# Gelu by its tanh form, four fetches at a time, on VectorE and ScalarE

## The reference, cut to what matters

```python
g = jax.nn.softmax(top_s, axis=-1).astype(hb.dtype)
u = jnp.take(expert_u, idx, axis=0)
act = jax.nn.gelu(jnp.einsum("thkd,td->thk", u, hb))
vv = jnp.take(expert_v, idx, axis=0)
return jnp.einsum("thk,thkd->td", g * act, vv)
```

## Time and profile before

| | |
|---|---|
| median of 3 runs | 2028.38 us (2023.79 to 2033.21) |
| profiled execution | 2043.05 us, its span 2041.0 us |
| PE busy | 1634.1 us (80%) |
| VectorE busy | 1205.5 us (59%) |
| ScalarE busy | 721.4 us (35%) |
| DMA moved | 718.22 MB, mean 352 GB/s |
| of it the indirect fetches | 604.02 MB, 72.2% of 16 engines' span |
| chain that ended last | DMA 42%, PE 29%, VectorE 14%, issue 8%, ScalarE 4% |

### The profile page before, as it was taken

One profiled execution on the slowest core, in us unless ns is written; L12 is line 12 of the kernel. 1 busy time (PEld: TensorE's weight loads), 2 busy tenths in 40 slices (PEclk: granted clock), 3 DMA queues, 4 the chain that ended last, 5 costly groups with the idle time before them and its releaser, 6 DMA issues.

```text
span 2041.0 us, 22251 instructions
## 1 busy us (share of the span) xinstructions
PE 1634.1 (80%) x7437; PEld 784.4 (38%) x7437; DVE 1205.5 (59%) x3104; ACT 721.4 (35%) x2231; POOL 628.5 (31%) x584
## 2 busy tenths in 40 slices
PE   6999998977887789889889677676676776767776
PEld 4775786844443345445355321121121121211221
DVE  2425112787787675544677667777766666665554
ACT  2215201353266543322423243333333333333332
POOL 0000000143331343333333254444343444343431
PEclk8999999998977799999999999998998999999989
DMA  9557520699995799999998699999999999999996
GB/s 399 205 189 269 194 91 21 247 375 362 395 366 220 291 411 421 421 421 411 414 389 322 253 423 421 421 422 421 422 421 421 421 422 421 422 420 422 422 420 249
DMA packets 100386, 718.22 MB, mean 352 GB/s; under 512 B 11488, under 2 KB 11504, under 8 KB 13488
## 3 DMA queue, kind: packets, MB, share of 16 engines
q0 software_dynamic: 82944, 604.02, 72.2%
q1 hardware_dynamic: 16464, 110.43, 13.9%
q10 hardware_dynamic: 864, 2.36, 0.3%
HBM read 712.04 MB, written 4.73 MB: 351 GB/s over the span
## 4 chain that ended last, share of the span: by engine, by line
DMA 42%; PE 29%; DVE 14%; issue 8%; ACT 4%; POOL 3%; SPq 0%; another core or an unknown queue 0%; DVEq 0%; POOLq 0%; ACTq 0%
DMA ring<-in_expert_uv_dram,uidx 41%; PE ps L877 7%; PE ps L612 6%; DVE ring L1544 6%; PE ps L736 4%; POOL ring L480 3%; PE ps L757 3%; PE ps L742 2%; DMA ring<-in_wpack_dram 1%; PE ps L608 1%; ACT wsel L1134 1%; PE ps L642 1%; PE ps L857 1%; ACT wdiag L1139 1%; DVE left L1447 1%
## 5 line engine op out<-in xcount | busy, mean ns | idle before, releaser
L877 PE MATMUL ps<-ring,wdiag 128*32 128x512 f32 x2304 | 814.1, 673 | 282.4 <-ACT wdiag L1139 206.6
L480 POOL DMA_INDIRECT ring<-in_expert_uv_dram,uidx x576 | 627.2, 1089 | 1328.8 <-PE ps L877 853.3
L1544 DVE CUSTOM_DVE_ANT_0 ring<-ring,mA 128x1024 f32<-128x1024 f32 x576 | 699.4, 1223 | 472.7 <-DMA ring<-in_expert_uv_dram,uidx 456.6
L877 PEld LDWEIGHTS ps<-ring,wdiag 128*32 128x32 f32 x2304 | 170.6, 118 | 846.1 <-ACT wdiag L1139 455.2
L1132 ACT ACTIVATE gel<-act_in 128x1 f32<-128x1 f32 x576 | 116.6, 202 | 854.7 <-DVE act_in L1544 839.8
L1139 ACT ACTIVATE wdiag<-repeat,wsel 128x32 f32<-128x32 f32 x576 | 185.1, 321 | 18.8
L1134 ACT ACTIVATE wsel<-gel,gsel 128x1 f32<-128x1 f32 x576 | 169.7, 295 | 18.7
L612 PE MATMUL ps<-hB,ring 128*128 128x320 f32 x320 | 93.1, 440 | 0.7 <-ACT convB L991 0.7
L612 PE MATMUL ps<-hA,ring 128*128 128x256 f32 x320 | 73.5, 391 | 6.8 <-DVE qB L1264 3.7
L795 PE MATMUL ps<-hB,ring 128*128 128x320 f32 x256 | 77.2, 455 | 0.0
L736 PE MATMUL ps<-hB,ring 128*128 128x320 f32 x256 | 73.2, 439 | 0.0
(11 more groups left out here) (241 smaller groups left out, 1593.7 us busy)
## 6 DMA issues: line engine op xcount, KB each, us to landing
ring<-in_wpack_dram SPq DMA_DIRECT2D x96, 1024.0 KB, 5.8
ring<-in_expert_uv_dram,uidx POOLq DMA_INDIRECT x576
xB<-in_x_b_dram SPq DMA_DIRECT2D x2, 1280.0 KB, 19.3
o_y_p<-mA ACTq DMA_DIRECT2D x16, 128.0 KB
xA<-in_x_a_dram SPq DMA_DIRECT2D x1, 1024.0 KB, 5.2
bias<-in_bias_dram SPq DMA_DIRECT2D x1, 1024.0 KB, 32.0
o_v_p<-kv SPq DMA_DIRECT2D x4, 256.0 KB, 13.4
o_k_p<-xB SPq DMA_DIRECT2D x4, 256.0 KB, 7.5
```

Source lines behind the costliest of these rows:

```text
L480: nc.gpsimd.indirect_dma_start(out=ring[:, slot, :], out_offset=None, in_=ins["expert_uv"], in_offset=bass.IndirectOffsetOnAxis(ap=uidx[:, ...
L877: mm = nc.tensor.matmul(pY[c * GT:(c + 1) * GT, half, :], wdiag[:, n % NDIAG, :], ring[:, ROW[n][0], D + half * 512:D + (half + 1) * 512], ...
L1544: nc.vector.tensor_tensor_reduce(r, r, h2n[:, g % 2, :], 1.0, 0.0, ALU.mult, ALU.add, act_in[:, g % 2, j:j + 1]).then_inc(s["dot"], 1)
```

## The change

The three ScalarE instructions of each fetch become work on a row of four fetches r (fetches 4r to 4r+3).

- VectorE, in entry 4r+3 behind the dot (`inner_row`): square, half of x times gate, factor, argument; four instructions on 128x4, two of them behind a wait for the one before.
- ScalarE, in entry 4r+4 (`tanh_row`): one Tanh on 128x4.
- VectorE, in entry 4r+4 behind the dot of fetch 4r+4 (`weight_row`): (tanh + 1) times half x times gate, one instruction on 128x4. It waits for the tanh.
- ScalarE, in entry 4r+5 (`spread_row`): the four diagonals, each as before.

TensorE, GpSimd, SyncE and the order are not touched. The folds of the row stay in TensorE's entry 4r+5. At the last row entry 576 has no dot. The buffers `gel` and `wsel` become two rows deep. ScalarE's waits for `placed_kept` go, since the dot of a row comes behind them anyway.

```diff
--- before.py
+++ after.py
@@ -20,6 +20,7 @@
 NKEY = 128
 TOPK = 16
 EPS = 1e-6
+GELU_A, GELU_C = 0.044715, 0.7978845608028654
 
 
 C_BADA, C_G1, C_G2, C_CW, C_CC, C_QG, C_KG, C_C = 0, 48, 56, 64, 76, 84, 85, 86
@@ -319,7 +320,7 @@
          "ada_ps", "ada_row", "ada_col", "mod", "x_loaded0", "x_loaded1", "x_again", "k_cache", "v_cache", "bias",
          "keys0", "keys1", "used",
          "shifted", "exp", "picked", "placed", "placed_kept",
-         "h2", "h2_kept", "dot", "gelu", "weight", "diag", "fold", "sum_kept", "joined", "scaled", "natural", "added", "stored",
+         "h2", "h2_kept", "dot", "inner", "tanh", "weight", "diag", "fold", "sum_kept", "joined", "scaled", "natural", "added", "stored",
          "gate_ps", "gate_sb", "v_out", "k_out", "state_ps", "state_row", "conv_out", "chain"]
 GROUP = ["sq", "sq_used", "mean", "inv", "root", "xn", "h_act", "h_dve", "z", "zsq", "zraw", "zsum", "zmean", "zinv", "zroot", "zqk", "za", "zd",
          "s_ps", "s_dve", "mx", "ex", "tp", "pt", "val", "on", "ot", "at", "kn_ps", "kn",
@@ -416,8 +417,8 @@
         uidx = sb("uidx", [P, 2, REP, GT], U32)
         gsel = sb("gsel", [P, 2, REP, GT])
         act_in = sb("act_in", [P, 2, GT])
-        gel = sb("gel", [P, GT])
-        wsel = sb("wsel", [P, GT])
+        gel = sb("gel", [P, 2, 4, REP])
+        wsel = sb("wsel", [P, 2, REP])
         wdiag = sb("wdiag", [P, NDIAG, GT])
         repeat = sb("repeat", [P, GT])
         stat = sb("stat", [P, 3, 2])
@@ -1121,23 +1122,18 @@
                         act.wait_ge(s["scaled"], GATED[n])
                     nc.scalar.copy(gate2, pG).then_inc(s["gate_sb"], 1)
 
-                def spread(n):
-                    g, j = n // GT, n % GT
-                    act.wait_ge(s["dot"], n + 1)
-                    p, a = TILES[g]
-                    if g == 0 and j % REP == 0:
-                        act.wait_ge(s["placed_kept"], nth(0, j // REP))
-                    if p and j == 0:
-                        act.wait_ge(s["placed_kept"], nth(p))
-                    nc.scalar.activation(gel[:, j:j + 1], act_in[:, g % 2, j:j + 1], ACT.Gelu_apprx_tanh).then_inc(s["gelu"], 1)
-                    act.wait_ge(s["gelu"], n + 1)
-                    nc.scalar.activation(wsel[:, j:j + 1], gel[:, j:j + 1], ACT.Identity,
-                                         scale=gsel[:, p % 2, a, j:j + 1]).then_inc(s["weight"], 1)
-                    act.wait_ge(s["weight"], n + 1)
-                    if n >= NDIAG:
-                        act.wait_ge(s["fold"], n - NDIAG + 1)
-                    nc.scalar.activation(wdiag[:, n % NDIAG, :], repeat[:, :], ACT.Identity,
-                                         scale=wsel[:, j:j + 1]).then_inc(s["diag"], 1)
+                def tanh_row(r):
+                    act.wait_ge(s["inner"], r + 1)
+                    nc.scalar.activation(gel[:, r % 2, 3, :], gel[:, r % 2, 2, :], ACT.Tanh).then_inc(s["tanh"], 1)
+
+                def spread_row(r):
+                    act.wait_ge(s["weight"], r + 1)
+                    for k in range(REP):
+                        n = REP * r + k
+                        if n >= NDIAG:
+                            act.wait_ge(s["fold"], n - NDIAG + 1)
+                        nc.scalar.activation(wdiag[:, n % NDIAG, :], repeat[:, :], ACT.Identity,
+                                             scale=wsel[:, r % 2, k:k + 1]).then_inc(s["diag"], 1)
 
                 def keep_sum(g):
                     act.wait_ge(s["fold"], GT * (g + 1))
@@ -1156,8 +1152,10 @@
                     act.dma_start(dst, prod[a * GT:(a + 1) * GT, :]).then_inc(s["stored"], 16)
 
                 def gather(n):
-                    if 1 <= n <= NG * GT:
-                        spread(n - 1)
+                    if n and n % REP == 0:
+                        tanh_row(n // REP - 1)
+                    if n > REP and n % REP == 1:
+                        spread_row(n // REP - 1)
                     m = n - 2
                     g, j = m // GT, m % GT
                     if j == 1 and g >= 1:
@@ -1544,6 +1542,26 @@
                     nc.vector.tensor_tensor_reduce(r, r, h2n[:, g % 2, :], 1.0, 0.0,
                                                    ALU.mult, ALU.add, act_in[:, g % 2, j:j + 1]).then_inc(s["dot"], 1)
 
+                def inner_row(r):
+                    g, j = r * REP // GT, r * REP % GT
+                    p, a = TILES[g]
+                    x, b = act_in[:, g % 2, j:j + REP], gel[:, r % 2]
+                    dve.wait_ge(s["dot"], REP * (r + 1))
+                    cd.did(nc.vector.tensor_tensor(b[:, 0, :], x, x, ALU.mult))
+                    cd.did(nc.vector.scalar_tensor_tensor(b[:, 1, :], x, 0.5, gsel[:, p % 2, a, j:j + REP], ALU.mult, ALU.mult))
+                    settle()
+                    cd.did(nc.vector.tensor_scalar(b[:, 0, :], b[:, 0, :], GELU_C * GELU_A, GELU_C, ALU.mult, ALU.add))
+                    settle()
+                    nc.vector.tensor_tensor(b[:, 2, :], b[:, 0, :], x, ALU.mult).then_inc(s["inner"], 1)
+
+                def weight_row(r):
+                    b = gel[:, r % 2]
+                    dve.wait_ge(s["tanh"], r + 1)
+                    if r >= 2:
+                        dve.wait_ge(s["diag"], REP * (r - 1))
+                    nc.vector.scalar_tensor_tensor(wsel[:, r % 2, :], b[:, 3, :], 1.0, b[:, 1, :],
+                                                   ALU.add, ALU.mult).then_inc(s["weight"], 1)
+
                 def scale(g):
                     p, a = TILES[g]
                     part = slice(a * GT, (a + 1) * GT)
@@ -1562,6 +1580,10 @@
                 def gather(n):
                     if n < NG * GT:
                         dot(n)
+                    if n < NG * GT and n % REP == REP - 1:
+                        inner_row(n // REP)
+                    if n and n % REP == 0:
+                        weight_row(n // REP - 1)
                     m = n - 2
                     g, j = m // GT, m % GT
                     if j == 7 and g >= 1:
```

## The result

The changed kernel takes 2152.90 us (median of 4 runs, 2146.05 to 2156.36) against 2030.80 us for the kernel before (median of 4, 2023.79 to 2045.03): a ratio of 1.0588, interval 1.0524 to 1.0652. It is slower by 122 us. The forecast was +45 and the range ended at 2105, so the direction held and the size did not.

What follows compares the result with a forecast made beforehand. Transfers bound the kernel from 1170 us, transfers and TensorE two earlier stretches, rounds of waits the other 395 us. Terms 8 + 5 - 5 + 10 + 25 + 2 = +45 on 2028.4 gave 2073 us; range 2020 to 2105.

Steps and rivals of the forecast that it cites:

- the refill: From 1170 us on, behind the last head: eleven slots with 6 us spare per row, so 0 us there.
- The time of a release: Every row: first fold 2.1 us behind the next row's dot, four folds over at 5.0, first slot free at 4.0.
- the bound of 16 us: Upper bound for 380 to 480 us: folds at the lower clock, taking twice as long.
- The cover of eight slots: 480 to 580 and 705 to 1000 us: transfers' cover falls to nothing, +5 (0 to 11) and +10 (0 to 24).
- rival C: The ring of slots runs dry, 24 and 11 us in the full stretches: +70, 2098 us; chance 0.12.
- The retrieval of group 1: 1000 to 1170 us: folds wait for dots behind a head's choice, delaying projections and `key_scores`: +25, bounds +8 and +33.
- the stand ahead of MAX8 in the fifth head: Retrieval of group 1: VectorE's wait ahead of the next choice would be longer than the 5.09 us before.
- The first heads: 380 to 480 us: folds behind the next dot delay `key_scores` 2.1 us a head for four heads: +8, bounds 0 and 16.
- Attention: 580 to 705 us: -10 table loads, -8 folds side by side, +10 later diagonals, +3 VectorE: -5, bounds -24 and above +10.
- rival D: Tanh needs its own table load after Exp, so 580 to 705 us stands at +5: 2083 us; chance 0.05.
- VectorE: Five small added instructions, about 0.9 us per four fetches, hidden behind 1170: +3 in attention, 2 in the retrieval.
- From 248 on: Fetches alone, paced by transfers: 0 us, plus 2 us behind the last dot for the last row.

Runs made afterwards that it cites:

- e11: The changed kernel with seven slots in turn for fetches instead of eight: 2263.73 us, ratio 1.1168 to the kernel before.
- e12: The changed kernel with nine slots for fetches instead of eight and two instead of three for weight blocks: 2109.40 us, ratio 1.0396 to the kernel before.
- e10: The changed kernel with TensorE's folds for fetches 188 to 227 moved from entry 4r+5 to 4r+7: 2119.39 us, ratio 1.0445 to the kernel before.
- e2: The kernel before with Tanh in place of Gelu, one fetch at a time, the rest of Gelu left out: 2034.21 us, ratio 0.9981.
- e5: The kernel before with five VectorE instructions added per row, writing a buffer that nobody reads: 2051.32 us, ratio 1.0070.

## Why the prediction was wrong in size

The mechanism and its place in the order were read rightly: no fold of a row ahead of the next dot, ring and `key_scores` behind it. No ACT_TABLE_LOAD is left in the attention stretch, as forecast. What failed is the sizes: the loss was put at 45 us and is 122, two of its terms came out above their upper bounds, and the refill, put at 0, at 14.

- **The time of a release.** The prediction had the first fold 2.1 us behind the dot, 2.9 us for four, the first slot free at 4.0 and the next issue at 4.3. Measured: 1.7 us to the first fold in most rows, a little better. Then there are two kinds of row. In the one the four folds take 1.9 to 2.5 us, and where the first starts at 1.7 the issue comes 3.9 us behind the dot, earlier than forecast. In the other, nearly always behind a stand of TensorE, they take 3.5 to 4.3 us, and the issue mostly comes at 5.2 to 6.1. From 88 to 184 eleven of 24 rows took over 3 us, from 184 to 232 ten of twelve; the mean from dot to issue is 4.9 and 6.1 us. So the step that failed is the price of a row of folds: the 1.94 us of the earlier trace rows is that of folds between projections, and it was used for rows that the change itself puts behind a stand. Only the bound of 16 us named the slower case, for the first stretch and no other. One row of each kind:

```profile
1021.61 2.54 PE L878 MATMUL ps<-ring,wdiag 128*32 128x512 f32 x16 [2.06 <-ACT wdiag L1135]
...
1023.78 1.56 POOL L481 DMA_INDIRECT ring<-in_expert_uv_dram,uidx  x1 [6.83 <-PE ps L878]
```

```profile
1714.07 3.89 PE L878 MATMUL ps<-ring,wdiag 128*32 128x512 f32 x16 [4.40 <-ACT wdiag L1135]
...
1717.92 1.45 POOL L481 DMA_INDIRECT ring<-in_expert_uv_dram,uidx  x1 [4.77 <-PE ps L878]
```

  In the first the issue comes 2.17 us behind the start of the folds, as forecast (1.9 + 0.3), in the second 3.85.
- **The cover of eight slots**, +10 for 88 to 184 and +5 for 24 to 56. Measured +19.0 and +11.5, rival C's mechanism (24 and 11). The 0.4 us a row was a choice, with the round of 11.7 us against 11.8 available. In the refill that round is 1275.50 - 1263.94 = 11.6 us, so it was right as a sum: a later release (5.6) met a shorter flight (6.0 instead of 7.4). The 7.4 was one reading and no floor; the trace of before has 6.2 us between fetches 100 and 183. But a round that equals what is available leaves nothing for rows that come late, and a mean over rows that vary lies above it. e11 and e12 show how steep it is here: +111 and -43 us for a slot.
- **The retrieval of group 1**, +25, measured +39.2. The effect was seen, but counted in full (8.1 us) for two heads and at 0.3 to 2 us for the others, whose rows "end in the dots anyway". In the trace of before nine of the twelve rows had begun to fold ahead of the next dot; two were read, and the rest was guessed. From one choice to the next (the first MAX8 of each head) the round of the second head takes 24.7 us instead of 16.0 and that of the fifth 25.1 instead of 19.4: +8.7 and +5.7 where 8.1 each was forecast. The other five rounds make +15.1, and the rows ahead of the first choice +9.8 (41.8 us from the dot of 184 instead of 32.0): 24.9 together, where 7 for the folds and 2 for VectorE were forecast. So it is less the two rows read than the rest. In the changed kernel TensorE stands 4.6 us or more in ten of twelve. One sign failed with it: the stand ahead of MAX8 in the fifth head is not longer than 5.09 us but 2.61, since VectorE now stands 6.05 us for fetch 216 first. e10 moves ten rows out of the way and gets 34.7 us of the stretch back.
- **The refill**, taken as 0 "from 1170", measured +14.0. This step was simply wrong: eleven slots are in turn only from fetch 237, and the first row there starts with an empty ring. The head of the stretch was read by its mean.
- **The first heads**, +8, measured +12.7. The four rounds that were priced, from the dot of 4 to that of 20, take 69.0 us instead of 60.1: +8.9, right as a size, though with folds of 4.1 us that begin 0.4 earlier. The rest is behind them, from the dot of 20 to that of 24 (11.7 us instead of 7.8): fetch 24 is issued at 483.73, and VectorE stands 4.79 us for its landing, where it stood none before. That is a slot that comes late, and the sum had no term for it.
- **Attention**, -5, measured +6.7. The loads were to give 10 us; the 45 that e2 removes in the whole kernel (68 were there, 23 are left), 58 us of ScalarE's time, give 2.3 us. So the chain's 8.2% was no saving; that the same engines waited for something else behind a load is the likely reason, and not shown. This also disposes of rival D, since Tanh needs no load of its own. The page "ScalarE: Activation LUTs" of the Trainium skill has the sharing of the table right ("Table sets: the hidden batching unit"), as e2's rows show. Its 2.66 us for a switch ("What ACT_TABLE_LOAD costs") is made of a load of about 1283 ns, which the rows show, and a drain, which they don't: there is 0.1 us of idle time ahead of eight loads. How attention's +6.7 is made up stays open: the parts here are as large as the difference between two executions.
- **VectorE**, +5 in all (3 in attention, 2 in the retrieval), measured +15 (e5). Its instructions cost 0.16 us each as forecast. e5's stretches differ from those of before by +3.7 in the first, +6.4 in attention and +2.8 in the last, the others by less or below nothing; with 5 us between executions, where the 15 lie isn't settled.
- **From 248 on**, 0, and 2 for the last row: measured +3.5. Right.
- **The range.** It treated the terms as if they missed independently. But one quantity, how late a row's slots come free, sits in five of them, and they move together. Their upper bounds, 16 + 11 + 10 + 24 + 33 = 94, and the missed refill of 14 make 108, near the 110 by which the two profiled executions differ; the measured five make 89.

## What to carry to other kernels

When a result is handed over a batch later, ask first which buffers the batch holds meanwhile and how many microseconds are left between their release and the next need; the instructions that the batching saves are the smaller figure (here 2 us of table loads against 107 us of delay). Where several terms of a sum hang on one release time, move them together when the range is made. And a wait in an in-order engine costs by what is queued behind it: if it can't be made shorter, put the engine's own ready work ahead of it, and give the ring a slot for the delay.
